# Sums of squares in a delta-rule encoder: two one-pass products of rounded parts in place of one full-precision product

## The chip, the cores and the metric

The kernel is one program on one core of a Trainium2 chip. The metric is the device time of one execution in microseconds (us). The engines are named as the profile names them: PE is TensorE (PEld its weight loads), DVE is VectorE, ACT is ScalarE, POOL is GpSimd, SP is SyncE.

## The reference

A two-layer encoder trunk over 512 positions of width 1024. Layer 1 has a gated DeltaNet with 8 heads of width 128, beside a cross-attention into 256 memory rows; layer 2 has sliding-window attention and the same cross-attention; each layer ends with a SwiGLU. What matters here is one head of the DeltaNet:

```python
qkv = silu(causal_depthwise_conv(qkv, conv_w))
q = l2_norm(q.reshape(B, S, 8, 128)) * 128 ** -0.5       # x * rsqrt(sum(x * x) + EPS)
k = l2_norm(k.reshape(B, S, 8, 128))
o = gated_delta_rule(q, k, v, g, beta)                   # chunks of 64, WY form
o = rms_norm(o, out_norm) * silu(z)                      # x * rsqrt(mean(x * x) + EPS)
```

Each head thus needs three sums of squares over its 128 channels for each of the 512 positions: of its keys, of its queries, and of its output.

## The kernel before

Activations lie with channels on the partitions and positions along the free axis, so a sum over channels is a product with a matrix of ones: `sq(ONES)` (128 by 128 ones, f32) times the squares (128x512, f32) gives the sum on every partition. The weight tiles of all projections come as a stream of blocks through a ring of four. ACT rounds a block to its upper part (`upper`, type fp32r), POOL subtracts for the lower part (`lower`), and PE makes three one-pass products for each 128-wide slice (`product`, line 594: upper by upper, upper weight by lower activation, lower weight by upper activation). A product of two f32 operands appears in the trace as two records for each instruction.

Each engine has its own program, written out by hand, and semaphores order them. Heads follow one another; PE does the delta rule of head h (`delta`, from line 696 on) and puts slices of the projections of head h+1 between its dependent steps: `fill(a, b)` stands for slices a to b-1 of the 32 (8 for each of q, k, v and gate), three one-pass products each. Head 7 has no next head; its only filling is the first memory-query tile, so `fill` does nothing there beyond slice 7.

Around the boundary of two heads PE's order is: in the loop over the four tiles of 128 positions (t = 0 to 3) the products of state and values, with the key sums of head h+1 (line 694) in tile 3; then `fill(30, 32)`; the output sums of head h (line 820); then, in the next `delta`, the query sums (line 703), four transposes of v (line 606, called from `delta`), two products with 64 rows that spread decay and beta over the partitions (line 717, "picks"), `fill(0, 2)`, four transposes of the normed keys (606 again), the keys' Gram product (line 727), `fill(2, 9)`, and the first step of the triangular inverse (line 735).

What feeds them: ACT squares k into `PM` (`square_k`) and q into `E0` (`square_q`), squares the output out of PSUM bank `D[5]` into `E1`, and takes Ln and Exp of the sums (`rr_k`, and in `delta`). Its Silu needs another table than Ln and Exp, so there is a table load behind `silu_v` (line 1326). DVE evacuates the value tiles in the t loop (`v_done`), updates `state` (`s_done`), then works on the output (`o_t1`), on the normed keys (`normed_k`, `kn_done`), on `PM` = keys times beta (`kb_done`, from the second pick), on the decay matrix (`dm_pre`) and on the first triangular factors (`z_done`). A helper's line stands for many operations: 1139 is ACT's `a`, 1578, 1581, 1584 and 1587 are DVE's multiply, subtract, fused operation and copy.

Of the kernel before, what the change touches and what calls it, by code (L numbers as in the profile page):

```python
# [126 lines left out]
def yoco_kernel(nc, x, mem, w_stream, w_out, w_down, w_ba, cols_in, squares_in, dist_in, out):  # L127
    with ExitStack() as ctx:
# [3 lines left out]
        def sem(name):  # L132
            return ctx.enter_context(nc.semaphore(name))
# [18 lines left out]
        class S:  # L152
# [48 lines left out]
            cv_conv = sem("cv_conv")  # L201
            c_ready = sem("c_ready")
            sz_done = sem("sz_done")
            sq_done = sem("sq_done")
            ss_done = sem("ss_done")
            rr_ln = sem("rr_ln")
# [35 lines left out]
            s_done = sem("s_done")  # L242
            o_done = sem("o_done")
            osq = sem("osq")
            oss = sem("oss")
            o_ln = sem("o_ln")
            o_rstd = sem("o_rstd")
# [66 lines left out]
        def due(n):  # L314

            return not isinstance(n, int) or n > 0
# [16 lines left out]
        def w(i):  # L333
            return ws[:, i, :]
# [4 lines left out]
        def sq(i):  # L339
            return sq_c[:, i, :]  # L340
# [26 lines left out]
        def psum(b, n=512):  # L367
            return bank[:, b, 0:n]
# [71 lines left out]
        def tz_count(k, g, first_only=False):  # L440

            if k < LEVELS - 2:
                return 2 * (k - 1) + g + 1
            if k == LEVELS - 2:
                return 2 * (LEVELS - 3) + 3 * g + (1 if first_only else 3)
            return 2 * (LEVELS - 3) + 6 + g + 1

        def row_cols(half):

# [135 lines left out]
        def _(pe):  # L585
# [110 lines left out]
            def delta(h, fill):  # L696

                if h == 0:
                    key_sums_dn(0)
                pe.wait_ge(S.sq_done, 2 * h + 2)  # L700
                if due(h):
                    pe.wait_ge(S.at_done, h)
                nc.tensor.matmul(psum(D[0]), sq(ONES), w(E0), start=True, stop=True).then_inc(S.ss_done, 1)
# [4 lines left out]
                transposes4(D[4], CV).then_inc(S.vtr_done, 1)  # L708

                if h == 0:  # L710
                    pe.wait_ge(S.rw_done, 2)
                    pe.wait_ge(S.pick_done, 1)
                if due(h):
                    pe.wait_ge(S.o_ln, h)
                    pe.wait_ge(S.v_done, NT * h)
                for half in range(2):
                    nc.tensor.matmul(psum(D[2 + half]), pick(h, half), rows(half), start=True, stop=True
                                     ).then_inc(S.gb_done, 1)
                fill(0, 2)
                pe.wait_ge(S.kn_done, h + 1)  # L720
                if due(h):
                    pe.wait_ge(S.o_t1, h)
# [414 lines left out]
        def _(act):  # L1137
            def a(out_, in_, func, **kw):
                return nc.scalar.activation(out_, in_, func, **kw)  # L1139
# [125 lines left out]
            def silu_v(h):  # L1265
                act.wait_ge(S.acc_free, TILE0["dn"] + 4 * h + 3)
                a(w(CV), w(CV), ACT.Silu).then_inc(S.c_ready, 1)

            def square_k(h):
                act.wait_ge(S.c_ready, 2 * h + 1)  # L1270
                if due(h):
                    act.wait_ge(S.tz_mm, 12 * h)
                a(w(PM), w(CK), ACT.Square).then_inc(S.sq_done, 1)

            def square_q(h):

                if due(h):
                    act.wait_ge(S.o_done, h)
                a(w(E0), w(CQ), ACT.Square).then_inc(S.sq_done, 1)

            def rr_k(h):
                act.wait_ge(S.ss_done, 2 * h + 1)
# [10 lines left out]
            def delta(h, fill, following):  # L1293
                act.wait_ge(S.gb_done, 2 * h + 1)
                a(w(EG), psum(D[2]), ACT.Exp).then_inc(S.eg_done, 1)
                act.wait_ge(S.ss_done, 2 * h + 2)
                a(w(E0), psum(D[0]), ACT.Ln, bias=col("eps")).then_inc(S.rr_ln, 1)
                at_once(act)
                act.wait_ge(S.dm_pre, h + 1)
                for t in range(NT):  # L1300
                    nc.scalar.activation(tt(DD, t), tt(DD, t), ACT.Exp, bias=dn(TMP1)[:, h, t:t + 1]
                                         ).then_inc(S.dm_done, 1)
                act.wait_ge(S.rr_ln, 2 * h + 2)
                a(psum(D[0]), w(E0), ACT.Exp, scale=-0.5, bias=col("ln_q")).then_inc(S.rr_done, 1)
# [269 lines left out]
        def _(dve):  # L1574
# [14 lines left out]
            def hi(tile_):  # L1589
                return act_hi[:, tile_, :].bitcast(F32)  # L1590
# [104 lines left out]
            def normed_k(h):  # L1695
                dve.wait_ge(S.rr_done, 2 * h + 1)
                mul(w(KN), w(CK), psum(D[1])).then_inc(S.kn_done, 1)

            def o_finish(h):
                dve.wait_ge(S.o_rstd, h + 1)  # L1700
                dve.wait_ge(S.o_t1, h + 1)
                mul(w(SZ), w(SZ), w(E1)).then_inc(S.o_t2, 1)

            def delta(h, fill, following=True):
# [66 lines left out]
                for t in range(NT):  # L1771
                    dve.wait_ge(S.v_mm, NT * h + t + 1)
                    cp(tt(E0, t), bank[:, D[3], 0:P]).then_inc(S.v_done, 1)
                    if t == NT - 1:
                        break
                    fill(2, t + 1)
                    dve.wait_ge(S.s_mm, 3 * h + t + 1)
                    if t == 0:
                        cp(state[:], bank[:, D[4], 0:P]).then_inc(S.s_done, 1)
                    else:  # L1780
                        dve.wait_ge(S.s_done, 3 * h + t)
                        stt(state[:], state[:], dn(GL)[:, h, t:t + 1], bank[:, D[4], 0:P], ALU.mult, ALU.add
                            ).then_inc(S.s_done, 1)
                fill(3)
                dve.wait_ge(S.osq, h + 1)
# [287 lines left out]
```

## Time and profile before

| | us |
|---|---|
| median of 3 runs (lowest, highest) | 1559.68 (1555.99, 1560.15) |
| the profiled execution, its own time | 1560.31 |
| its span, first to last instruction | 1558.5 |
| PE busy in the span | 1514.9 (97%) |
| DVE, ACT, POOL busy | 568.3, 601.8, 559.7 |
| mean granted clock of TensorE | 0.990 |

The span is 1.8 us shorter than the profiled execution's own time; differences are made in the span and carried to the median. Matmuls are pipelined: the start of one to the start of the next is what one costs, its own duration is longer than that.

### The profile page before, as it was taken

The page shows a single profiled execution, that of the slowest core. Times are in us where ns is not written, and L with a number is a line of the kernel's source. Part 1 is how long each engine was busy: PE and PEld are TensorE (multiplying, and loading weights), DVE is VectorE, ACT ScalarE, POOL GpSimd, SP SyncE. Part 2 cuts the span into 40 slices and gives each one's busy share as a digit, 9 for nine tenths or more (in the row PEclk, how much of TensorE's full clock was granted, in tenths as well). Part 3 has the DMA queues.
Part 4 walks back from the last instruction along what each step waited for, and adds up shares of the span by engine and source line. Part 5 has one row for each costly group of instructions (what it writes and reads, how often), then busy time and mean ns, then how long its engine had stood idle before and what let it go on. Part 6 is the DMA issues. An engine that isn't in the chain of part 4 may idle for free.

```text
span 1558.5 us, 23359 instructions
## 1 busy us (share of the span) xinstructions
PE 1514.9 (97%) x8956; PEld 1217.7 (78%) x8956; DVE 568.3 (36%) x1037; ACT 601.8 (39%) x998; POOL 559.7 (36%) x270
## 2 busy tenths in 40 slices
PE   6889999999999999999999999999999999999998
PEld 6867777777777788888888887777788888888887
DVE  2345556555564322221122224665432222112210
ACT  5534444334443433222232334675533232223221
POOL 4532221332312344444443443122244444444442
PEclk9999999999999999999999999999999999999999
DMA  6322101111101133223322233111123322332232
GB/s 238 119 66 70 42 29 54 55 55 42 49 15 31 53 113 108 101 71 103 117 88 102 68 118 102 41 38 31 41 81 109 108 92 83 110 107 83 91 86 80
DMA packets 39227, 124.36 MB, mean 80 GB/s; under 512 B 4192, under 2 KB 5472, under 8 KB 39136
## 3 DMA queue, kind: packets, MB, share of 16 engines
q1 hardware_dynamic: 38976, 122.81, 24.3%
q8 instruction: 66, 1.08, 0.3%
q10 hardware_dynamic: 160, 0.26, 0.1%
q14 instruction: 25, 0.20, 0.0%
HBM read 120.70 MB, written 2.10 MB: 79 GB/s over the span
## 4 chain that ended last, share of the span: by engine, by line
PE 93%; DVE 3%; ACT 2%; issue 1%; DMA 0%; POOL 0%; SPq 0%; DVEq 0%; ACTq 0%
PE bank L594 74%; ACT ws L1139 2%; PE bank L757 2%; PE bank L775 1%; PE bank L1073 1%; PE bank L778 1%; DVE act_lo L1584 1%; PE bank L940 1%; PE bank L899 1%; DVE ws L1587 1%; PE bank L1097 1%; PE bank L1084 1%; PE bank L740 1%; PE bank L812 1%; PE bank L786 1%
## 5 line engine op out<-in xcount | busy, mean ns | idle before, releaser
L541 POOL TENSOR_TENSOR w_lo<-w_raw,w_hi 128x1024 fp32r<-128x1024 f32 (+1 forms) x250 | 539.5, 2174 | 822.1 <-ACT w_hi L1139 822.0
L594 PE MATMUL bank<-act_hi,w_hi 128*128 128x512 f32 (+1 forms) x1776 | 711.5, 401 | 6.7 <-DVE act_lo L1584 2.6
L594 PE MATMUL bank<-act_hi,w_lo 128*128 128x512 f32 (+1 forms) x1776 | 681.7, 384 | 0.0
L594 PE MATMUL bank<-act_lo,w_hi 128*128 128x512 f32 (+1 forms) x1776 | 680.7, 383 | 0.0
L594 PEld LDWEIGHTS bank<-act_hi,w_hi 128*128 128x128 f32 x1776 | 336.3, 189 | 79.9 <-issue 13.2
L594 PEld LDWEIGHTS bank<-act_hi,w_lo 128*128 128x128 f32 x1776 | 336.1, 189 | 66.2
L594 PEld LDWEIGHTS bank<-act_lo,w_hi 128*128 128x128 f32 x1776 | 336.7, 190 | 62.3 <-issue 5.8
L1139 ACT ACTIVATE w_hi<-w_raw 128x1024 fp32r<-128x1024 f32 (+1 forms) x250 | 230.5, 953 | 88.8 <-PE bank L594 86.6
L1578 DVE TENSOR_TENSOR ws<-bank,ws 128x512 f32<-128x512 f32 x110 | 75.9, 690 | 336.9 <-PE bank L594 326.9
L1139 ACT ACTIVATE ws<-ws 128x512 f32<-128x512 f32 (+2 forms) x135 | 87.1, 647 | 155.4 <-DVE ws L1578 108.3
L1864 DVE TENSOR_TENSOR xT<-xT,bank 128x512 f32<-128x512 f32 (+1 forms) x48 | 33.0, 688 | 256.9 <-PE bank L594 256.9
L1139 ACT ACTIVATE act_hi<-ws 128x512 fp32r<-128x512 f32 (+1 forms) x52 | 32.8, 630 | 238.5 <-DVE ws L1578 238.5
L1139 ACT ACTIVATE ws<-bank 128x512 f32<-128x512 f32 (+2 forms) x64 | 41.8, 653 | 118.6 <-PE bank L991 44.9
L1587 DVE COPY ws<-bank 128x128 f32<-128x128 f32 (+4 forms) x94 | 40.0, 440 | 100.6 <-PE bank L594 51.7
L1242 ACT ACTIVATE ws<-bank,cols 128x512 f32<-128x512 f32 x24 | 16.5, 686 | 136.4 <-PE bank L594 136.4
L1584 DVE SCALAR_TENSOR_TENSOR ws<-bank,cols,ws 128x510 f32<-128x510 f32 (+3 forms) x80 | 59.6, 745 | 12.5 <-ACT ws L1242 10.8
L555 POOL TENSOR_TENSOR act_lo<-ws,act_hi 128x512 f32 (+1 forms) x8 | 10.3, 1291 | 148.6 <-ACT act_hi L1139 148.6
L1581 DVE TENSOR_TENSOR ws<-ws,bank 128x256 f32<-128x256 f32 (+2 forms) x112 | 39.3, 363 | 46.5 <-PE bank L778 44.3
L1139 ACT ACTIVATE ws<-xT 128x512 f32<-128x512 f32 (+1 forms) x24 | 15.2, 632 | 105.4 <-DVE xT L1864 105.4
L1139 ACT ACTIVATE ws<-bank,cols 128x512 f32<-128x512 f32 (+1 forms) x52 | 33.9, 651 | 51.0 <-PE bank L624 14.7
L1581 DVE TENSOR_TENSOR act_lo<-ws,act_hi 128x512 fp32r<-128x512 f32 (+1 forms) x44 | 30.5, 693 | 34.5 <-ACT act_hi L1139 34.5
L775 PEld LDWEIGHTS bank<-ws 64*64 64x64 f32 x640 | 31.8, 134 | 13.3 <-issue 12.8
(158 smaller groups left out, 1183.2 us busy)
## 6 DMA issues: line engine op xcount, KB each, us to landing
w_raw<-w_stream SPq DMA_DIRECT2D x154, 512.0 KB, 3.2
w_raw<-w_out SPq DMA_DIRECT2D x32, 384.0 KB, 3.1
w_raw<-w_down SPq DMA_DIRECT2D x32, 384.0 KB, 3.1
w_raw<-w_down SPq DMA_DIRECT2D x32, 320.0 KB, 3.1
ws<-x_in SPq DMA_DIRECT2D x1, 2048.0 KB, 8.4
ws<-mem_in SPq DMA_DIRECT2D x2, 512.0 KB, 4.8
out<-ws SPq DMA_DIRECT2D x1, 1024.0 KB, 4.2
out<-ws SPq DMA_DIRECT2D x1, 768.0 KB, 3.7
```

The costliest lines, as they stand in the source:

```text
L541: nc.gpsimd.tensor_tensor(w_lo[:, s, 0:width * P], w_raw[:, s, 0:width * P], w_hi[:, s, 0:width * P].bitcast(F32), ALU.subtract).then_inc( ...
L594: mm = nc.tensor.matmul(acc, wt[:, c % RING, wsl], at[:, act0(k0 + k), off:off + n], start=(start and k == 0 and m == 0), stop=(stop and k ...
L740: mm = nc.tensor.matmul(bank[:, D[0], t * P:(t + 1) * P], tt(KN, t), tt(QN, t), start=True, stop=True)
L757: mm = nc.tensor.matmul(bank[half_rows(r), D[3 - g], HB * i:HB * (i + 1)], diag(MM, t, r, r), packed(TT, t, r), start=True, stop=True)
L775: nc.tensor.matmul(bank[half_rows(r), D[4 + g], HB * i:HB * (i + 1)], packed(TT, t, r, 1), packed(PM, t, r), start=True, stop=True)
L1139: return nc.scalar.activation(out_, in_, func, **kw)
L1242: nc.scalar.activation(w(CQ + j), psum(j % 2), ACT.Copy, scale=conv_w(h, j, 3)).then_inc(S.cv_tap, 1)
L1578: return V.tensor_tensor(out_, x_, y_, ALU.mult)
L1581: return V.tensor_tensor(out_, x_, y_, ALU.subtract)
L1584: return V.scalar_tensor_tensor(out=out_, in0=x_, scalar=scalar, in1=y_, op0=op0, op1=op1)
L1587: return V.tensor_copy(out_, x_)
L1864: V.tensor_tensor(xT[:, k, :], xT[:, k, :], psum(j), ALU.add).then_inc(S.acc_free, 1)
```

## The change

For heads 1 to 7's keys and queries and for heads 0 to 6's output, squares are no longer multiplied in f32. ACT writes the squares into a PSUM bank, ACT copies them with rounding into an fp32r tile (the upper part), DVE subtracts that from the squares into a second fp32r tile (the lower part), and PE adds two one-pass products with a rounded matrix of ones. The keys' and the queries' parts share one pair of tiles. The query sums and the transposes of v move from the head's start to the end of the head before, ahead of the output sums; the picks move behind `fill(0, 2)`; `fill(2, 3)` moves between the key transposes and the Gram product. On ACT `square_q` moves ahead of `silu_v`. Head 0's sums and head 7's output sums are made as before.

```diff
+        SUM_T, OHI_T, OLO_T = KT + CAT - 1, 16, 17
+        ones_r = act_lo[:, 18, 0:P]
@@ tensor
+            def two_part_sums(acc, upper_, lower_):
+                nc.tensor.matmul(psum(acc), ones_r, upper_, start=True, stop=False)
+                return nc.tensor.matmul(psum(acc), ones_r, lower_, start=False, stop=True)
             def key_sums_dn(h):
                 pe.wait_ge(S.sq_done, 2 * h + 1)
-                nc.tensor.matmul(psum(D[1]), sq(ONES), w(PM), start=True, stop=True).then_inc(S.ss_done, 1)
...
+                two_part_sums(D[1], act_hi[:, SUM_T, :], act_lo[:, SUM_T, :]).then_inc(S.ss_done, 1)
+            def query_sums_dn(h):
                 pe.wait_ge(S.sq_done, 2 * h + 2)
...
+                two_part_sums(D[0], act_hi[:, SUM_T, :], act_lo[:, SUM_T, :]).then_inc(S.ss_done, 1)
+            def value_transposes(h):
                 pe.wait_ge(S.c_ready, 2 * h + 2)
                 if due(3 * h):
                     pe.wait_ge(S.s_done, 3 * h)
                 transposes4(D[4], CV).then_inc(S.vtr_done, 1)
+            def delta(h, fill):
+                if h == 0:
+                    key_sums_dn(0)
+                    query_sums_dn(0)
+                    value_transposes(0)
+                fill(0, 2)
                 if h == 0:
                     pe.wait_ge(S.rw_done, 2)
-                    pe.wait_ge(S.pick_done, 1)
+                    pe.wait_ge(S.pick_done, 2)
...
-                fill(0, 2)
                 pe.wait_ge(S.kn_done, h + 1)
...
                 transposes4(D[5], KN).then_inc(S.ktr_done, 1)
+                fill(2, 3)
...
-                fill(2, 9)
+                fill(3, 9)
...
                 fill(30, 32)
-                pe.wait_ge(S.osq, h + 1)
-                nc.tensor.matmul(psum(D[2]), sq(ONES), w(E1), start=True, stop=True).then_inc(S.oss, 1)
+                if h + 1 < DN_HEADS:
+                    query_sums_dn(h + 1)
+                    value_transposes(h + 1)
...
+                pe.wait_ge(S.osq_lo, h + 1)
+                two_part_sums(D[2], act_lo[:, OHI_T, :], act_lo[:, OLO_T, :]).then_inc(S.oss, 1)
@@ scalar
             def square_k(h):
...
+                act.wait_ge(S.tz_mm, 12 * h)
+                a(psum(D[1]), w(CK), ACT.Square).then_inc(S.sq_hi, 1)
+                act.wait_ge(S.sq_hi, 4 * h - 3)
+                act.wait_ge(S.ss_done, 2 * h)
+                a(act_hi[:, SUM_T, :], psum(D[1]), ACT.Copy).then_inc(S.sq_hi, 1)
             def square_q(h):
...
+                act.wait_ge(S.at_done, h)
+                a(psum(D[0]), w(CQ), ACT.Square).then_inc(S.sq_hi, 1)
+            def round_q(h):
+                act.wait_ge(S.sq_hi, 4 * h - 1)
+                act.wait_ge(S.ss_done, 2 * h + 1)
+                a(act_hi[:, SUM_T, :], psum(D[0]), ACT.Copy).then_inc(S.sq_hi, 1)
@@ scalar, delta
                 if following:
+                    square_q(h + 1)
                     silu_v(h + 1)
                 act.preload_act_table_set("natural_log_exp_and_others")
+                if following:
+                    round_q(h + 1)
                 act.wait_ge(S.o_done, h + 1)
-                a(w(E1), psum(D[5]), ACT.Square).then_inc(S.osq, 1)
                 if following:
-                    square_q(h + 1)
+                    a(psum(D[2]), psum(D[5]), ACT.Square).then_inc(S.osq, 1)
+                    act.wait_ge(S.osq, 2 * h + 1)
+                    a(act_lo[:, OHI_T, :], psum(D[2]), ACT.Copy).then_inc(S.osq, 1)
...
             conv_tile(0, 1)
+            a(ones_r, sq(ONES), ACT.Copy).then_inc(S.pick_done, 1)
@@ vector
+            def split_k(h):
+                dve.wait_ge(S.sq_hi, 4 * h - 2)
+                sub(act_lo[:, SUM_T, :], psum(D[1]), hi(SUM_T)).then_inc(S.sq_done, 1)
+            def split_q(h):
+                dve.wait_ge(S.sq_hi, 4 * h)
+                sub(act_lo[:, SUM_T, :], psum(D[0]), hi(SUM_T)).then_inc(S.sq_done, 1)
+            def split_o(h):
+                dve.wait_ge(S.osq, 2 * h + 2)
...
+                sub(act_lo[:, OLO_T, :], psum(D[2]), act_lo[:, OHI_T, :].bitcast(F32)).then_inc(S.osq_lo, 1)
@@ vector, delta, in and behind the loop over t
+                    if following and t == 1:
+                        split_k(h + 1)
+                if following:
+                    split_q(h + 1)
+                    split_o(h)
                 fill(3)
```

## Rows read from the trace of the kernel before

**Rows 1.** The page: the chain that ended last by engine, and two costly groups.
```profile
PE 93%; DVE 3%; ACT 2%; issue 1%; DMA 0%; POOL 0%; SPq 0%; DVEq 0%; ACTq 0%
...
L1139 ACT ACTIVATE act_hi<-ws 128x512 fp32r<-128x512 f32 (+1 forms) x52 | 32.8, 630 | 238.5 <-DVE ws L1578 238.5
...
L1581 DVE TENSOR_TENSOR act_lo<-ws,act_hi 128x512 fp32r<-128x512 f32 (+1 forms) x44 | 30.5, 693 | 34.5 <-ACT act_hi L1139 34.5
```

**Rows 2.** Busy time by stretch: PE, PEld, DVE, ACT, POOL, PE clock, DMA share, GB/s.
```profile
354.00:400.00 46.00, 45.94 (x444) 35.02 (x443) 26.24 (x61) 19.42 (x30) 11.93 (x6) 1.00 0.14 47
...
446.00:480.00 34.00, 30.76 (x367) 25.08 (x366) 20.38 (x52) 12.07 (x20) 2.49 (x2) 0.90 0.01 1
...
1080.00:1100.00 20.00, 18.48 (x92) 14.09 (x92) 6.81 (x11) 8.12 (x17) 4.90 (x2) 0.83 0.07 20
```

**Rows 3.** Timeline of PE across the boundary of heads 4 and 5: start, duration.
```profile
349.48 1.02 PE L694 MATMUL bank<-ws,sq_c 128*128 128x512 f32 x2
350.34 0.38 PE L802 MATMUL bank<-state,ws 128*128 128x128 f32 x2
...
351.49 0.39 PE L815 MATMUL bank<-ws 128*128 128x128 f32 x2
...
353.10 1.02 PE L820 MATMUL bank<-ws,sq_c 128*128 128x512 f32 x2
353.96 1.02 PE L703 MATMUL bank<-ws,sq_c 128*128 128x512 f32 x2
354.82 0.60 PE L606 MATMUL bank<-sq_c,ws 128*128 128x128 f32 x4
355.35 0.50 PE L717 MATMUL bank<-act_hi 64*128 64x512 f32 x2
355.78 0.50 PE L594 MATMUL bank<-act_hi,w_hi 128*128 128x512 f32 x1
356.12 0.39 PE L594 MATMUL bank<-act_lo,w_hi 128*128 128x512 f32 x1
...
357.27 0.60 PE L606 MATMUL bank<-sq_c,ws 128*128 128x128 f32 x4
357.71 1.06 PE L727 MATMUL bank<-ws 128*128 128x128 f32 x8
358.52 0.48 PE L594 MATMUL bank<-act_hi,w_hi 128*128 128x512 f32 x1
358.84 0.39 PE L594 MATMUL bank<-act_lo,w_hi 128*128 128x512 f32 x1
...
363.17 0.39 PE L594 MATMUL bank<-act_hi,w_lo 128*128 128x512 f32 x1
363.49 0.68 PE L735 MATMUL bank<-sq_c,ws 64*64 64x64 f32 x16
```

**Rows 4.** Timeline of ACT at the same boundary.
```profile
349.08 0.63 ACT L1139 ACTIVATE ws<-ws 128x512 f32<-128x512 f32 x1 [3.86 <-DVE ws L1584]
349.73 1.28 ACT L1326 ACT_TABLE_LOAD   x1
351.91 0.60 ACT L1139 ACTIVATE ws<-bank 128x512 f32<-128x512 f32 x1 [0.90 <-PE bank L815]
...
352.93 0.68 ACT L1139 ACTIVATE ws<-bank,cols 128x512 f32<-128x512 f32 x1
353.64 0.60 ACT L1139 ACTIVATE bank<-ws 128x512 f32<-128x512 f32 x1
```

**Rows 5.** Timeline of DVE at the same boundary.
```profile
346.84 0.35 DVE L1584 SCALAR_TENSOR_TENSOR state<-state,dn_s,bank 128x128 f32<-128x128 f32 x1 [0.29 <-PE bank L812]
348.09 0.29 DVE L1587 COPY ws<-bank 128x128 f32<-128x128 f32 x1 [0.91 <-PE bank L802]
...
356.00 0.69 DVE L1578 TENSOR_TENSOR ws<-ws,bank 128x512 f32<-128x512 f32 x1 [0.75 <-PE bank L717]
...
360.50 0.42 DVE L1581 TENSOR_TENSOR ws<-sq_c,bank 128x256 f32<-128x256 f32 x1
```

More of the change, by code:

```diff
@@ L203, in yoco_kernel @@
             sz_done = sem("sz_done")
+            sq_hi = sem("sq_hi")
             sq_done = sem("sq_done")
@@ L244, in yoco_kernel @@
             osq = sem("osq")
+            osq_lo = sem("osq_lo")
             oss = sem("oss")
@@ L689, in half_tiles @@
                 return range(NT // 2 * g, NT // 2 * (g + 1))
+            def two_part_sums(acc, upper_, lower_):
+                nc.tensor.matmul(psum(acc), ones_r, upper_, start=True, stop=False)
+                return nc.tensor.matmul(psum(acc), ones_r, lower_, start=False, stop=True)
             def key_sums_dn(h):
                 pe.wait_ge(S.sq_done, 2 * h + 1)
-                nc.tensor.matmul(psum(D[1]), sq(ONES), w(PM), start=True, stop=True).then_inc(S.ss_done, 1)
-            def delta(h, fill):
                 if h == 0:
-                    key_sums_dn(0)
+                    nc.tensor.matmul(psum(D[1]), sq(ONES), w(PM), start=True, stop=True).then_inc(S.ss_done, 1)
+                    return
+                two_part_sums(D[1], act_hi[:, SUM_T, :], act_lo[:, SUM_T, :]).then_inc(S.ss_done, 1)
+            def query_sums_dn(h):
                 pe.wait_ge(S.sq_done, 2 * h + 2)
-                if due(h):
-                    pe.wait_ge(S.at_done, h)
-                nc.tensor.matmul(psum(D[0]), sq(ONES), w(E0), start=True, stop=True).then_inc(S.ss_done, 1)
+                if h == 0:
+                    nc.tensor.matmul(psum(D[0]), sq(ONES), w(E0), start=True, stop=True).then_inc(S.ss_done, 1)
+                    return
+                two_part_sums(D[0], act_hi[:, SUM_T, :], act_lo[:, SUM_T, :]).then_inc(S.ss_done, 1)
+            def value_transposes(h):
                 pe.wait_ge(S.c_ready, 2 * h + 2)
@@ L708, in delta @@
                 transposes4(D[4], CV).then_inc(S.vtr_done, 1)
+            def delta(h, fill):
+                if h == 0:
+                    key_sums_dn(0)
+                    query_sums_dn(0)
+                    value_transposes(0)
+                fill(0, 2)
                 if h == 0:
                     pe.wait_ge(S.rw_done, 2)
-                    pe.wait_ge(S.pick_done, 1)
+                    pe.wait_ge(S.pick_done, 2)
                 if due(h):
@@ L817, in delta @@
                 fill(30, 32)
-                pe.wait_ge(S.osq, h + 1)
-                nc.tensor.matmul(psum(D[2]), sq(ONES), w(E1), start=True, stop=True).then_inc(S.oss, 1)
+                if h + 1 < DN_HEADS:
+                    query_sums_dn(h + 1)
+                    value_transposes(h + 1)
+                if h + 1 == DN_HEADS:
+                    pe.wait_ge(S.osq, 2 * h + 1)
+                    nc.tensor.matmul(psum(D[2]), sq(ONES), w(E1), start=True, stop=True).then_inc(S.oss, 1)
+                    return
+                pe.wait_ge(S.osq_lo, h + 1)
+                two_part_sums(D[2], act_lo[:, OHI_T, :], act_lo[:, OLO_T, :]).then_inc(S.oss, 1)
             proj_dn(0, 0)
@@ L1270, in square_k @@
                 act.wait_ge(S.c_ready, 2 * h + 1)
-                if due(h):
-                    act.wait_ge(S.tz_mm, 12 * h)
-                a(w(PM), w(CK), ACT.Square).then_inc(S.sq_done, 1)
-            def square_q(h):
-                if due(h):
-                    act.wait_ge(S.o_done, h)
-                a(w(E0), w(CQ), ACT.Square).then_inc(S.sq_done, 1)
+                if isinstance(h, int) and h == 0:
+                    a(w(PM), w(CK), ACT.Square).then_inc(S.sq_done, 1)
+                    return
+                act.wait_ge(S.tz_mm, 12 * h)
[3 more added lines that the diff above has]
+                a(act_hi[:, SUM_T, :], psum(D[1]), ACT.Copy).then_inc(S.sq_hi, 1)
+            def square_q(h):
+                if isinstance(h, int) and h == 0:
+                    a(w(E0), w(CQ), ACT.Square).then_inc(S.sq_done, 1)
+                    return
+                act.wait_ge(S.at_done, h)
[4 more added lines that the diff above has]
+                a(act_hi[:, SUM_T, :], psum(D[0]), ACT.Copy).then_inc(S.sq_hi, 1)
             def rr_k(h):
@@ L1324, in delta @@
                 if following:
+                    square_q(h + 1)
                     silu_v(h + 1)
                 act.preload_act_table_set("natural_log_exp_and_others")
+                if following:
+                    round_q(h + 1)
                 act.wait_ge(S.o_done, h + 1)
-                a(w(E1), psum(D[5]), ACT.Square).then_inc(S.osq, 1)
                 if following:
-                    square_q(h + 1)
+                    a(psum(D[2]), psum(D[5]), ACT.Square).then_inc(S.osq, 1)
+                    act.wait_ge(S.osq, 2 * h + 1)
+                    a(act_lo[:, OHI_T, :], psum(D[2]), ACT.Copy).then_inc(S.osq, 1)
+                else:
+                    a(w(E1), psum(D[5]), ACT.Square).then_inc(S.osq, 1)
+                if following:
                     rr_k(h + 1)
@@ L1697, in normed_k @@
                 mul(w(KN), w(CK), psum(D[1])).then_inc(S.kn_done, 1)
+            def split_k(h):
[6 more added lines that the diff above has]
+                dve.wait_ge(S.osq, 2 * h + 2)
+                if due(h):
+                    dve.wait_ge(S.oss, h)
+                sub(act_lo[:, OLO_T, :], psum(D[2]), act_lo[:, OHI_T, :].bitcast(F32)).then_inc(S.osq_lo, 1)
             def o_finish(h):
@@ L1783, in delta @@
                             ).then_inc(S.s_done, 1)
+                    if following and t == 1:
+                        split_k(h + 1)
+                if following:
+                    split_q(h + 1)
+                    split_o(h)
                 fill(3)
-                dve.wait_ge(S.osq, h + 1)
+                dve.wait_ge(S.osq, 2 * h + 1)
                 dve.wait_ge(S.sz_done, h + 1)
```

## The prediction

> **What bounds the kernel now.** I read the chain that ended last first: 93% of it lies on PE [rows 1]. Then busy time by stretch, to see whether that holds in the delta rule: in a stretch as long as one head PE is busy 45.94 of 46.00 us at a granted clock of 1.00, DVE 26.24 and ACT 19.42 [rows 2]. Then PE's timeline across the boundary of two heads, where the change sits; no row there shows idle time [rows 3]. So in heads 0 to 6 each 0.1 us taken off PE is gained, as long as nothing new arrives late. Head 7 is different: with little to fill in, PE is busy 30.76 of 34 us [rows 2]; its chain hangs on line 735, and PE is full up to there, so what is gained ahead of it counts.
>
> **PE, the three sums.** From the start of one f32 sum to the next instruction is 350.34 - 349.48, 353.96 - 353.10 and 354.82 - 353.96, each 0.86 us [rows 3]. A one-pass product of the same size: from 358.84 to 363.17 there are 19 steps, 4.33/19 = 0.228 us [rows 3]. Two are 0.455, so a sum gives back 0.405, three per boundary 1.215 us. There are seven boundaries.
>
> **PE, the changes of kind.** The first one-pass product after f32 work takes 358.84 - 358.52 = 0.32 us, 0.09 more than the others; after the picks with 64 rows it takes 356.12 - 355.78 = 0.34, 0.11 more; line 735, 64 rows, starts 0.32 after the last product, again 0.09; the v transposes ahead of the picks take 355.35 - 354.82 = 0.53, the same four of the keys ahead of f32 work 357.71 - 357.27 = 0.44, again 0.09. From one-pass work into f32 it costs nothing: 349.48 to 350.34 and 353.10 to 353.96 are equal, though only the second follows one-pass products [rows 3]. Counting the new order by these: new are the key sums between f32 products (0.09), the output sums after the v transposes (0.09), fill into picks (0.09), picks into key transposes (0.11, the nearest row is the one that leaves the picks), and key transposes into `fill(2, 3)` (0.09), together 0.47. Gone are transposes into picks (0.09) and picks into fill (0.11), 0.20. Net 0.27 lost per boundary, between 0.16 (leaving the picks into f32 free) and 0.38 (another 0.11 somewhere). A boundary gives 1.215 - 0.27 = 0.945, seven 6.6 us. Head 0 keeps its sums but has the new order: 0.09 + 0.09 + 0.11 + 0.09 - 0.20 = 0.18 lost. That leaves 6.4 us.
>
> **Queues and waits, on a clock of the row times.** Key sums: ACT sits idle for 3.86 us ahead of `silu_v` [rows 4], so the extra copy (0.63 by the fp32r group [rows 1]) costs nothing; the subtraction (0.69 by its group [rows 1]) comes behind the state update that ends at 347.19, ends at 347.9, and the next value copy was due at 348.09 [rows 5]. It fits by 0.2 us; if it did not, the key product with state behind it would be late by the same. PE wants it at 349.48. The key sums end 0.31 earlier than before (0.86 - 0.455 - 0.09), so everything behind them on PE stands 0.31 earlier: last output product 351.18, output sums' old place 352.79.
>
> Query sums: `square_q` is done long before. `round_q` can't start before the table load ends, 349.73 + 1.28 = 351.01 [rows 4]. Copy 0.60, subtraction 0.68 (the last value copy of DVE is done by then), hand-over 0.03 each (352.93 + 0.68 = 353.61, its dependent starts at 353.64 [rows 4]): ready at about 352.4. PE arrives at 352.79 and loads the weights of a product about one product ahead, 352.56. Covered by 0.2 us. Without that cover each 0.1 is lost seven times.
>
> Output sums: this is the tight one. The output was ready for ACT 351.91 - 351.49 = 0.42 after the start of line 815 [rows 3, 4], now 351.60. Square 0.60, copy 0.60, subtraction 0.69, three hand-overs of 0.03 to 0.05: 353.65 to 353.7. PE: 352.79 + 0.455 + 0.44 for the transposes = 353.68, the weight load a little earlier. I take 0.05 us of waiting per boundary, seven 0.35. Bounds: nothing (all covered), and 0.6 if each hand-over costs 0.16 (an estimate, five times the row), the two ACT operations cost the longest row, 0.68, and the weight load is exposed.
>
> Behind it: the sums land at 354.4, Ln takes 0.68, `o_ln` 355.15; PE reaches the picks at 355.7 and is not held. Key transposes at 356.2 need `kn_done`: `rr_k` slips behind the copy, 352.75 to 354.1, DVE does gate copy, `o_t1`, normed keys until 355.5. Free. The picks stand 0.37 later than before, so `kb_done` comes at 356.00 + 0.37 + 0.69 = 357.1 [rows 5]; the Gram product starts at 357.4, because `fill(2, 3)` stands ahead of it. The triangular start, before 360.50 + 0.42, slips to about 361.3; line 735, before 363.49, is reached at 362.45. So the cover of 2.6 us shrinks to 1.1 and holds, in head 7 too. The extra copy of ones sits on ACT at the start of the heads, off PE's path. No DMA moves; nothing is added on SP or POOL.
>
> **The sum.** 1560.31 - 6.4 + 0.35 = 1554.2 for the profiled execution's own time; the median of the runs is 0.63 below that execution, so 1553.6 us, 0.39% faster. What a measurement of this kernel can tell from no change is about 0.3%, 4.7 us.
>
> **A rule of the skill against the change.** The table load is a row of 1.28 us, and ACT is free when it ends: its next operation starts 0.90 us later, released by PE [rows 4]. The Trainium skill (ScalarE: Activation LUTs, "What ACT_TABLE_LOAD costs") gives about 1283 ns for the load and adds a drain of about 1380 ns to each switch of sets. If that drain came behind the load here, ACT would not be free before 352.39; the trace has it at work at 351.91, so the row speaks against it. By the rule both chains behind `round_q` would be late, see the third rival.
>
> **Rivals.**
> 1. The output chain is late by more than I say: 0.3 to 0.6 us of PE waiting at each boundary, 2.1 to 4.2 us in all. Then 1559.68 - 6.4 plus that, 1555.4 to 1557.5. For it: three dependent operations in place of one, with no slack. Against: the hand-overs in the rows are short. 18%.
> 2. The lower clock falls elsewhere. The stretch of head 7 has a mean clock of 0.90 over 34 us, the one from 1080 on 0.83 over 20 [rows 2]: each is 6.8 us at the 1.2 GHz level instead of 2.4, worth up to 3.4 us where PE is the bound. PE was busy 90% and 92% of these stretches, against all but 0.06 us in a head. Everything behind the heads moves by some 6 us, so one such place may vanish (1550.2, 7%) or one may be added (1557.0, 8%).
> 3. `round_q` waits for the end of ACT's change of tables longer than the row says. Place: the 0.90 us behind the load in each of seven boundaries. From 0.2 us on it is PE's wait for the query sums; at 1.4 us the query sums wait 1.2 and the output sums behind them 0.3 more, 10.5 us in all: 1563.8, slower by 0.26%. From about 0.9 us on the gain is gone. 2%.
> 4. The other side, by the clock: the new short waits of PE at the boundaries make the granted clock fall inside the heads, where it was 1.00 in the stretch shown and in the five like it [rows 2]. Price 3.4 us a time; with two the gain is gone, from four on (1567) it is slower by more than 0.3%. For it: head 7 shows that the clock does fall in this code once PE idles. Against: PE was busy 90% there, and the new waits are under 1% of a head. 5%.
> 5. The two products don't cost 0.455: an accumulating pair with weights of ones could take as long as f32 work. Then only the losses remain, about 1562. Line 594 is the same form of instruction and accumulates too, so 2%.
>
> **How the numbers follow.** My forecast, with its own range 1552.0 to 1555.5, 58%; rival 1 18%, rival 2 15%, rival 3 2%, rival 4 5%, rival 5 2%. Runs of one kernel spread over 4 us (1555.99 to 1560.15), which widens each. The range 1549.5 to 1558.8 takes in the forecast, rival 1 and most of rival 2, and leaves the slow cases and the far ends. Faster by over 0.3% (below 1555.0): most of the forecast, the better half of rival 2, a little of rival 1, 0.64. Within 0.3%: the rest of these and some of 3 to 5, 0.29. Slower 0.07.
>
> **What would show it.** Right: the sums as two records of 0.228 us from start to start; a head's period 0.9 to 1.0 us shorter; no waiting ahead of the query sums, up to 0.1 ahead of the output sums, with the lower part's subtraction named as releaser; line 735 not waiting. Wrong: a row of idle time on PE at the output sums of 0.3 or more, at the picks for the output's Ln, or at the Gram product for the keys times beta; a value copy of DVE in tile 2 that starts late behind the keys' subtraction; or a clock under 1.00 between 124 and 446 us.

## The result, and the profile after

The changed kernel takes 1549.83 us (median of 7 runs, 1542.53 to 1551.69), the kernel before 1559.57 in its 7 runs; the ratio is 0.993, with a 95% interval from 0.9918 to 0.9943. I forecast 1553.6, 6.1 us less; it is 9.7 less. By the ratio the time is 1548.8, a little under the low end of the range (1549.5). The profiled execution took 1550.04 us, span 1548.2. One run of a later version, `pair_twice` below, took 2148.07 us at a mean granted clock of 0.656 and is left out of its ratio.

In the timeline of PE of the changed kernel, line 756 is the old line 735, and lines 698 and 699 are the two products of a sum. These rows are the boundary of heads 4 and 5, and the line 756 of the head before:

```profile
312.80 0.68 PE L756 MATMUL bank<-sq_c,ws 64*64 64x64 f32 x16
...
344.03 0.38 PE L833 MATMUL bank<-ws 128*128 128x128 f32 x2
344.25 0.39 PE L836 MATMUL bank<-ws 128*128 128x128 f32 x2
344.47 0.39 PE L815 MATMUL bank<-ws 128*128 128x128 f32 x2
344.62 0.47 PE L698 MATMUL bank<-act_hi,act_lo 128*128 128x512 f32 x1
344.93 0.39 PE L699 MATMUL bank<-act_lo 128*128 128x512 f32 x1
345.16 0.38 PE L823 MATMUL bank<-state,ws 128*128 128x128 f32 x2
...
347.91 0.39 PE L698 MATMUL bank<-act_hi,act_lo 128*128 128x512 f32 x1
348.14 0.39 PE L699 MATMUL bank<-act_lo 128*128 128x512 f32 x1
348.38 0.60 PE L611 MATMUL bank<-sq_c,ws 128*128 128x128 f32 x4
348.74 0.50 PE L698 MATMUL bank<-act_lo 128*128 128x512 f32 x1
349.07 0.39 PE L699 MATMUL bank<-act_lo 128*128 128x512 f32 x1
349.31 0.39 PE L599 MATMUL bank<-act_hi,w_hi 128*128 128x512 f32 x1
...
350.46 0.39 PE L599 MATMUL bank<-act_hi,w_lo 128*128 128x512 f32 x1
350.78 0.50 PE L738 MATMUL bank<-act_hi 64*128 64x512 f32 x2
351.21 0.66 PE L611 MATMUL bank<-sq_c,ws 128*128 128x128 f32 x4
351.62 0.48 PE L599 MATMUL bank<-act_hi,w_hi 128*128 128x512 f32 x1
351.94 0.39 PE L599 MATMUL bank<-act_lo,w_hi 128*128 128x512 f32 x1
...
357.51 0.68 PE L756 MATMUL bank<-sq_c,ws 64*64 64x64 f32 x16
```

The head is 357.51 - 312.80 = 44.71 us long. Before, one head further on, it was 409.41 - 363.49 = 45.92, from the last row of [rows 3] to this one:

```profile
409.41 0.68 PE L735 MATMUL bank<-sq_c,ws 64*64 64x64 f32 x16
```

So a boundary gives back 1.21 us, not 0.9. No row of PE at the boundary has idle time. On ACT and DVE the new chain takes 2.00 us from the start of the output's square (346.74) to the start of the product on PE (348.74). The forecast's terms for it (0.60, 0.60, 0.69 and three hand-overs of 0.03 to 0.05) add up to 1.98 to 2.04.

```profile
344.30 0.63 ACT L1167 ACTIVATE ws<-ws 128x512 f32<-128x512 f32 x1 [2.77 <-DVE ws L1632]
344.95 1.28 ACT L1367 ACT_TABLE_LOAD   x1
346.24 0.60 ACT L1167 ACTIVATE act_hi<-bank 128x512 fp32r<-128x512 f32 x1
346.74 0.59 ACT L1167 ACTIVATE bank<-bank 128x512 f32<-128x512 f32 x1
347.36 0.60 ACT L1167 ACTIVATE act_lo<-bank 128x512 fp32r<-128x512 f32 x1
```

```profile
346.87 0.69 DVE L1629 TENSOR_TENSOR act_lo<-bank,act_hi 128x512 fp32r<-128x512 f32 x1 [1.00 <-ACT act_hi L1167]
347.99 0.69 DVE L1629 TENSOR_TENSOR act_lo<-bank,act_lo 128x512 fp32r<-128x512 f32 x1 [0.42 <-ACT act_lo L1167]
```

The output's lower part is ready at 347.99 + 0.69 = 348.68, and the first product of the output sums starts at 348.74. The table load starts 0.02 us behind the Silu ahead of it, and the copy that follows starts 0.01 us behind the load; the drain of some 1380 ns that the Trainium skill adds (ScalarE: Activation LUTs, "What ACT_TABLE_LOAD costs") does not show in this trace.

The difference of the two spans by stage, each from the same instruction in both timelines (the last start of a stage is the first of the next):

| stage | before | after | difference |
|---|---|---|---|
| start to the first sum of head 0 | 123.38 | 123.51 | +0.13 |
| from there to line 735 / 756 of head 0 | 10.51 | 10.45 | -0.06 |
| from there to the same line of head 7 | 320.78 | 312.32 | -8.46 |
| from there to the first memory scores | 32.45 | 30.62 | -1.83 |
| from there to the end | 1071.35 | 1071.34 | -0.01 |

The first line can't be put down to the change: the stage holds no edited product of PE, and its length lies between 120.6 and 124.5 us in the fourteen profiles of this document. The second is, since head 0 has the new order with its old sums:

```profile
123.38 1.12 PE L694 MATMUL bank<-ws,sq_c 128*128 128x512 f32 x2 [0.81 <-ACT ws L1139]
```

```profile
123.51 1.12 PE L705 MATMUL bank<-ws,sq_c 128*128 128x512 f32 x2 [0.81 <-ACT ws L1167]
...
133.96 0.68 PE L756 MATMUL bank<-sq_c,ws 64*64 64x64 f32 x16
```

The fourth line was not in the forecast's sum. PE's work there is the same; the clock is not. One row by stretch for the changed kernel, against the row of the same stretch in [rows 2] with its clock of 0.90:

```profile
446.00:480.00 34.00, 30.28 (x365) 23.65 (x364) 18.19 (x46) 10.96 (x16) 8.39 (x5) 1.00 0.04 11
```

### The profile page after: what moved, and what is told of

The parts are those of the page before. It is cut to its first block, busy times and chain, and to the rows that moved or that the text cites. A ratio compares the mean times of both kernels' runs of the same rounds, so it can differ in the third digit from the quotient of the medians.

```text
span 1548.2 us, 23430 instructions
## 1 busy us (share of the span) xinstructions
PE 1503.3 (97%) x8956; PEld 1212.6 (78%) x8956; DVE 581.3 (38%) x1058; ACT 613.2 (40%) x1020; POOL 559.7 (36%) x270
## 4 chain that ended last, share of the span: by engine, by line
PE 93%; DVE 3%; ACT 2%; issue 1%; DMA 0%; POOL 0%; SPq 0%; DVEq 0%; ACTq 0%
PE bank L599 74%; PE bank L778 2%; ACT ws L1167 2%; PE bank L796 2%; PE bank L1101 1%; PE bank L799 1%; DVE act_lo L1632 1%; PE bank L968 1%; PE bank L927 1%; DVE ws L1635 1%; PE bank L1125 1%; PE bank L761 1%; PE bank L611 1%; PE bank L919 1%; PE bank L957 1%
## 5 line engine op out<-in xcount | busy, mean ns | idle before, releaser
L1167 ACT ACTIVATE ws<-ws 128x512 f32<-128x512 f32 (+2 forms) x121 | 78.4, 650 | 147.8 <-DVE ws L1626 108.7
L1167 ACT ACTIVATE ws<-bank 128x512 f32<-128x512 f32 (+2 forms) x57 | 37.5, 659 | 107.9 <-PE bank L1019 44.9
```

## The experiments

Two questions: why a boundary gives 1.21 us, and whether head 7's clock belongs to the change. "Period" is the distance of line 735 or its counterpart from one head to the next. Where times are compared, note what the stages show below: kernels differ by several us in the time behind the heads, where nothing was edited. So the periods decide, not the ratios. A table behind the shifted versions has every version's distance from line 735 or its counterpart in head 0 to that in head 7, which is seven boundaries.

**The order alone** (`order_f32`). The sums are single f32 products again, the order is the new one. Query squares go to `E1`, output squares to `E0`, and DVE has no parts to make.

```diff
-                nc.tensor.matmul(psum(acc), ones_r, upper_, start=True, stop=False)
-                return nc.tensor.matmul(psum(acc), ones_r, lower_, start=False, stop=True)
+                return nc.tensor.matmul(psum(acc), sq(ONES), upper_, start=True, stop=True)
...
-                    a(psum(D[2]), psum(D[5]), ACT.Square).then_inc(S.osq, 1)
-                    act.wait_ge(S.osq, 2 * h + 1)
-                    a(act_lo[:, OHI_T, :], psum(D[2]), ACT.Copy).then_inc(S.osq, 1)
+                    a(w(E0), psum(D[5]), ACT.Square).then_inc(S.osq, 2)
```

> The new order of the boundary with all sums still single f32 products: query sums and v transposes ahead of the output sums, picks behind fill(0, 2), fill(2, 3) ahead of the Gram product, no parts. Theory A (a change from f32 to one-pass work costs 0.09 us, as the prediction counted): a boundary loses 0.09 (fill into picks) + 0.11 (picks into transposes) + 0.09 (key transposes into fill) - 0.20 = 0.09 or more, so 0.6 to 1.5 us slower in the heads, period 46.0 to 46.1 against 45.92. Theory B (the 0.09 of the first one-pass product is given back by the last f32 product before it, which gets shorter by as much): period within 0.03 of 45.92. Clock: if the dip in head 7 went away through the new order, head 7 shows a clock of 1.00 here too; if through the shorter heads or by chance, that is open.

Measured: ratio 0.9967 (0.9952 to 0.9983), period 45.85 to 45.90; over seven boundaries 320.46 us against 320.78, so 0.05 less for each than before, where theory A has 0.09 or more added. PE's timeline of this kernel; line 755 is the old 735:

```profile
317.65 0.68 PE L755 MATMUL bank<-sq_c,ws 64*64 64x64 f32 x16
...
354.46 1.02 PE L698 MATMUL bank<-ws,sq_c 128*128 128x512 f32 x2
354.92 0.80 PE L599 MATMUL bank<-act_hi,w_hi 128*128 128x512 f32 x1
355.56 0.40 PE L599 MATMUL bank<-act_lo,w_hi 128*128 128x512 f32 x1
...
363.50 0.68 PE L755 MATMUL bank<-sq_c,ws 64*64 64x64 f32 x16
```

Here an f32 sum is followed by one-pass work, and its rows say how such a place is to be read: 0.46 us to the next start, then 0.64 for the first one-pass product, together 1.10. An f32 sum ahead of f32 work takes 0.86 [rows 3] and a one-pass product 0.228, together 1.09. What the first one-pass product seems to take longer, the f32 instruction before it takes less. Theory A is excluded. Theory B gives its mechanism, but it expected the period within 0.03 of 45.92, and it is 0.02 to 0.07 below: the new order is a small gain of its own, taken apart further below.

**More changes of kind** (`kinds`).

```diff
                     mm = nc.tensor.matmul(bank[:, D[0], t * P:(t + 1) * P], tt(KN, t), tt(QN, t), start=True, stop=True)
+                    if t < NT - 1:
+                        fill(9 + t, 10 + t)
                 mm.then_inc(S.gg_done, 1)
-                fill(9, 12)
```

> The changed kernel with one edit: the four f32 products of keys with queries are no longer in a row with fill(9, 12) behind them, but each of the first three is followed by one slice of the fill. Same work, three more changes of kind to one-pass and three back, in each of heads 0 to 6. Theory A: each costs 0.09, a head 0.27, seven heads 1.9 us; period 44.99 against 44.72. Theory B: nothing, period within 0.05 of 44.72.

Measured: ratio 0.9937 (0.9922 to 0.9953), period 44.70 to 44.73, that of the changed kernel. PE's timeline, line 761 being the f32 products and 599 the slices between them:

```profile
315.26 0.39 PE L761 MATMUL bank<-ws 128*128 128x128 f32 x2
315.40 0.47 PE L599 MATMUL bank<-act_hi,w_hi 128*128 128x512 f32 x1
315.71 0.40 PE L599 MATMUL bank<-act_lo,w_hi 128*128 128x512 f32 x1
315.94 0.40 PE L599 MATMUL bank<-act_hi,w_lo 128*128 128x512 f32 x1
316.18 0.38 PE L761 MATMUL bank<-ws 128*128 128x128 f32 x2
```

The f32 product takes 0.14 and the first slice product 0.31; together 0.45, as 0.22 and 0.23 do apart. The expectation miscounts: without the edit the four products have `fill(9, 12)` behind them, which is one change to one-pass and one back, so the edit makes three of one, two more of each kind and not three. Theory A then has 0.18 for a head and a period of 44.90, which is still far from the 44.73 measured at most. Two more changes of this form cost nothing.

**Every pair twice** (`pair_twice`).

```diff
                 nc.tensor.matmul(psum(acc), ones_r, upper_, start=True, stop=False)
+                nc.tensor.matmul(psum(acc), ones_r, lower_, start=False, stop=True)
+                nc.tensor.matmul(psum(acc), ones_r, upper_, start=True, stop=False)
                 return nc.tensor.matmul(psum(acc), ones_r, lower_, start=False, stop=True)
```

> The changed kernel with each pair of one-pass products made twice (the first result is overwritten by the second). If a pair costs 0.455 us, a boundary gets 3 x 0.455 = 1.37 us longer, period 46.08, and the time 9.6 us longer than the changed kernel, about that of the kernel before. If an accumulating pair cost more (rival 5), more. If PE waited for the output parts and not for its own work, less than 0.455 would show at the output sums.

Measured: period 46.05 to 46.09, and 321.84 us over seven boundaries against 312.32, so 1.36 more for each than the changed kernel, or 0.45 for a pair. That is the forecast's price, and the accumulating pair is no dearer. The ratio is 0.9975 (0.9965 to 0.9985): by its heads this kernel is 1 us slower than before, yet it was timed faster, and only 6.1 us slower than the changed kernel (1555.57 against 1549.46), not 9.6. Its profiled execution had a mean granted clock of 0.997, that of the kernel before 0.990; that is the warning given above.

**The keys alone** (`keys_only`), on the kernel before.

```diff
+                pe.wait_ge(S.sq_k, h)
+                nc.tensor.matmul(psum(D[1]), ones_r, act_hi[:, SUM_T, :], start=True, stop=False)
+                nc.tensor.matmul(psum(D[1]), ones_r, act_lo[:, SUM_T, :], start=False, stop=True).then_inc(S.ss_done, 1)
```

> The kernel before with the key sums of heads 1 to 7 alone as two one-pass products of parts; order, query sums and output sums as before. As the products measured (0.86 against 0.455, changes of kind free): 0.40 per boundary, period 45.52, 2.8 us in all. By the prediction's count of kinds 0.31 per boundary, period 45.61.

Measured: period 45.51 to 45.54, and 318.00 us over seven boundaries against 320.78, so 0.40 for one sum per head; by the count of kinds it would have been 0.31. The ratio is 0.9947 (0.9929 to 0.9965), more than these 2.8 us; in the profile the rest lies behind the heads.

**The output's lower part later** (`late_output`).

```diff
+                    a(act_lo[:, OHI_T, :], psum(D[2]), ACT.Copy).then_inc(S.pick_done, 1)
+                    act.wait_ge(S.pick_done, h + 3)
                     a(act_lo[:, OHI_T, :], psum(D[2]), ACT.Copy).then_inc(S.osq, 1)
```

> The changed kernel with a second rounding copy of the output's squares in front of the first, so the lower part comes about 0.60 us later. My forecast gave this chain no cover (0.05 us of waiting), so PE should wait 0.55 to 0.65 ahead of the output sums: period 45.3 against 44.72, about 4 us. If a cover of x was there, the wait is 0.60 - x. If the chain is not on PE's path at all, no difference.

Measured: ratio 0.9952 (0.9936 to 0.9967), period 45.33 to 45.37, over seven boundaries 4.44 us more than the changed kernel, 0.63 for each. The copy and its hand-over are 0.63 to 0.64. PE's timeline of this kernel:

```profile
350.49 0.60 PE L611 MATMUL bank<-sq_c,ws 128*128 128x128 f32 x4
351.48 0.50 PE L698 MATMUL bank<-act_lo 128*128 128x512 f32 x1 [0.39 <-DVE act_lo L1631]
```

DVE's subtraction is named as releaser, and the whole delay comes through. The idle figure of 0.39 is smaller than the loss, since it counts from the modelled end of the transposes; from start to start it is 0.99 here and 0.36 in the changed kernel. So the output chain of the changed kernel had no cover at all. The delay alone doesn't show that it had no waiting; the rows of the changed kernel do, to 0.02 us. In head 0 the same transposes stand ahead of `fill(0, 2)`, which waits for no such chain, and the distance to the second one-pass product is 0.67, against 0.69 at the boundary (349.07 - 348.38):

```profile
125.33 0.60 PE L611 MATMUL bank<-sq_c,ws 128*128 128x128 f32 x4
125.68 0.48 PE L599 MATMUL bank<-act_hi,w_hi 128*128 128x512 f32 x1
126.00 0.40 PE L599 MATMUL bank<-act_lo,w_hi 128*128 128x512 f32 x1
```

**Both kernels again** (`after_again`, `before_again`), unedited.

> The changed kernel unchanged, for the clock of head 7 and the size of the gain. If the gain is the heads' alone, 8.4 us (0.54%); in the first profile the dip of the clock in head 7 had gone as well, 1.8 us more. If that is by chance, this profile may show the dip again (span 1550), if it belongs to the change, it is gone here too.

> The kernel before, unchanged, for the clock of head 7. If the dip of the clock there belongs to the kernel before, it shows again, with 1.8 us between line 735 of head 7 and the first memory scores (32.4 against 30.6). If it comes by chance, it may be gone, 30.6.

Measured: the changed kernel 1549.46 us, ratio 0.9932 (0.9919 to 0.9946), period 44.71, stage behind line 756 of head 7 30.62, clock there 1.00. The kernel before 1561.14 us in one run, period 45.92, that stage 32.20 (455.80 to 488.00), clock 0.90:

```profile
446.00:480.00 34.00, 31.60 (x370) 25.37 (x368) 21.05 (x52) 12.56 (x20) 2.49 (x2) 0.90 0.01 1
```

Up to here it looked like a property of the change. But `order_f32` (32.21), `keys_only` (32.49) and `late_output` (32.23) had the dip, `kinds` (30.62) and `pair_twice` (30.59) had none, and PE's work in head 7 is the same in all. `late_output` is the changed kernel but for one copy: with all its one-pass sums in place the dip is there.

**The same heads, a little later** (`before_shift1`, `before_shift2`, `after_shift1`, `after_shift2`). Products of the identity with itself, once, in head 0: 5 in the first of each pair, 10 in the second.

```diff
+                if h == 0:
+                    pe.wait_ge(S.mv_done, 2 * MEM_HEADS)
+                    for _ in range(5):
+                        nc.tensor.matmul(bank[:, D[5], 0:P], sq(IDENT), sq(IDENT), start=True, stop=True)
```

> The kernel before with 5 more f32 products of the identity with itself (about 1.1 us of PE) once, in head 0 ahead of the key transposes; heads 1 to 7 unchanged, only later. If the dip of the clock in head 7 belongs to the work of the heads before it, it stays (32.2 to 32.5 us from line 735 of head 7 to the first memory scores). If it hangs on when head 7 falls, it may vanish (30.6).

> The same with 10 products (about 2.2 us), heads 1 to 7 unchanged. Vanishing of the dip in one of the two shifts would show that timing decides and not the change's one-pass sums; the dip in both leaves the question open.

> The changed kernel with 5 such products in head 0. If the change's own work keeps the clock up in head 7, it stays up here. If timing decides, the dip may come back, with 1.6 to 1.9 us.

> The changed kernel with 10 such products in head 0 (about 2.2 us of PE). If the change's own work keeps the clock up in head 7, it stays up here too. If timing decides, the dip may come back, with 1.6 to 1.9 us.

Measured: 1559.42 and 1556.81 us for the two on the kernel before, 1543.84 and 1548.02 for the two on the changed one, a run each. The stage behind line 735 / 756 of head 7 takes 30.62, 30.63, 30.62 and 30.62: the dip is gone in the kernel before, with heads 1 to 7 as they were (period 45.92 and 45.93). The row of `before_shift2`:

```profile
446.00:480.00 34.00, 30.26 (x372) 23.53 (x371) 21.79 (x53) 13.17 (x22) 2.50 (x2) 1.00 0.01 1
```

So the one-pass sums are not needed to lose the dip: the same heads come with it and without. One difference is left in this comparison: `before_again` was profiled on another chip than the shifted versions, and no profile of the unedited kernel before is known to be from theirs. But `order_f32` ran on that chip too and has the dip, so the chip alone doesn't decide. Nor does the place in the span decide alone: line 735 of head 0 starts at 134.98 in `before_shift1`, without the dip, and at 135.04 in `before_again`, with it. The dip did not come back in the changed kernel. The tail moves as well: from the first memory scores of layer 1's stage to those of layer 2's `after_shift1` takes 598.9 us, the changed kernel 603.4. A stretch of this tail in the changed kernel, and then in `after_shift1`:

```profile
1060.00:1080.00 20.00, 16.73 (x108) 12.78 (x107) 7.64 (x14) 9.85 (x26) 2.69 (x2) 0.83 0.15 41
```

```profile
1060.00:1080.00 20.00, 16.73 (x98) 12.87 (x97) 8.53 (x14) 10.46 (x26) 2.58 (x1) 1.00 0.08 20
```

All profiles by stage, in us. "Head 0 to 7" runs from line 735 or its counterpart in head 0 to that of head 7, "head 7" from there to layer 1's first memory scores, "tail" from these to layer 2's. Behind each of the last two stands how much of it had a granted clock of 1.2 GHz:

| version | head 0 to 7 | head 7 | at 1.2 GHz | tail | at 1.2 GHz |
|---|---|---|---|---|---|
| before | 320.78 | 32.45 | 6.8 | 603.4 | 13.7 |
| `before_again` | 320.76 | 32.20 | 6.8 | 603.4 | 10.2 |
| `before_shift1` | 320.77 | 30.62 | 0 | 603.2 | 10.2 |
| `before_shift2` | 320.85 | 30.63 | 0 | 600.6 | 6.8 |
| `order_f32` | 320.46 | 32.21 | 6.8 | 600.5 | 6.8 |
| `keys_only` | 318.00 | 32.49 | 6.8 | 600.7 | 6.8 |
| `late_output` | 316.76 | 32.23 | 6.8 | 603.3 | 10.2 |
| `pair_twice` | 321.84 | 30.59 | 0 | 598.9 | 3.4 |
| `kinds` | 312.36 | 30.62 | 0 | 603.2 | 10.2 |
| `head7_filled` | 312.26 | 30.33 | 0 | 603.4 | 10.2 |
| changed | 312.32 | 30.62 | 0 | 603.4 | 10.2 |
| `after_again` | 312.25 | 30.62 | 0 | 603.1 | 10.2 |
| `after_shift1` | 312.27 | 30.62 | 0 | 598.9 | 3.4 |
| `after_shift2` | 312.33 | 30.62 | 0 | 599.0 | 3.4 |

The tail's length goes with its time at the lower clock: 598.9 or 599.0 us with 3.4 us of it, 600.5 to 600.7 with 6.8, 603.1 to 603.4 with more. The several us by which whole runs of these kernels differ beyond their heads are of this size, and no edit stands there.

**Head 7 filled** (`head7_filled`). The second memory-query tile's slices go into head 7's last steps.

```diff
-                mem_project(layer, 1, range(KT // 2 if layer else 0, KT))
+                if layer:
+                    mem_project(layer, 1, range(KT // 2, KT))
...
-            delta(DN_HEADS - 1, lambda first, end: mem_project(0, 0, range(first, min(end, KT))) if first < KT else None)
+            def beside_last_head(first, end):
+                if first < KT:
+                    mem_project(0, 0, range(first, min(end, KT)))
+                elif 22 <= first < 30:
+                    mem_project(0, 1, range(first - 22, first - 21))
+            delta(DN_HEADS - 1, beside_last_head)
```

> The changed kernel with the second memory-query tile's 8 slices (24 products, 5.5 us) moved from behind head 7 into its last steps (one slice at each fill place from 22 on), where PE waits for DVE. Those steps get longer by what the idle time doesn't hold: in the other heads a step of two slices takes 2.5 us, without them 2.0 to 2.1, so about 2 us for eight; behind it 5.5 are gone, but the chain from output sums over Ln, Exp and the normed query stands bare, 2 to 3 us. I expect 0.5 to 2 us less than the changed kernel from line 756 of head 7 to the first memory scores (30.6), and the clock at 1.00 through head 7. If the clock's dip came from too little work of PE, it can't come here.

Measured: 1549.72 us, ratio 0.9933 (0.992 to 0.9947), no better than the changed kernel. To the first scores it takes 30.33 us, 0.3 less, where 0.5 to 2 was expected. PE now waits for the normed query, and the clock falls behind that wait:

```profile
477.21 3.68 PE L927 MATMUL bank<-kmem,ws 128*128 128x256 f32 x8 [2.70 <-DVE ws L1638]
```

```profile
471.00:476.00 5.00, 2.82 (x9) 1.24 (x7) 1.48 (x3) 2.84 (x5) 0.00 (x0) 1.00 0.01 3
476.00:481.00 5.00, 3.79 (x9) 2.97 (x10) 1.43 (x3) 1.52 (x3) 3.97 (x3) 0.66 0.00 0
```

The scores take 3.5 us from start to start, where the kernel before has 1.72 (487.12 to 488.84). The idle time was moved, not removed. Of the versions tried none is faster than the changed kernel by its heads.

## Why the prediction was off

**Right.** PE as the bound of heads 0 to 6, and the three sums as the gain: 0.86 against 0.455 us was measured as 0.45 for a pair (`pair_twice`) and 0.40 for one sum exchanged (`keys_only`). The key sums' and the query sums' parts were in time. Rivals 3, 4 and 5 did not come: the copy starts 0.01 us behind the table load, the clock stays at 1.00 in the heads, the pair is not dearer. The output chain was just in time: `late_output` gives its cover as nothing, and the rows leave at most 0.02 of waiting where I took 0.05, so rival 1 was one short delay away. The forecast's time for it, 353.65 to 353.7, is an error of addition: 351.60 + 0.60 + 0.60 + 0.69 and three hand-overs of 0.03 to 0.05 make 353.58 to 353.64, just ahead of PE's 353.68, as measured. Line 735 does not wait.

**The failed step: "PE, the changes of kind".** I read 0.09 us off each first one-pass product behind f32 work, and counted net 0.27 per boundary and 0.18 in head 0, 2.1 us in all. Measured, the whole loss against 1.215 is about 0.01 per boundary (1.215 - 1.21), and in head 0 there is none: from its first sum to line 735 / 756 it takes 10.45 us, 0.06 less than before. The new order alone takes 0.05 off a boundary (`order_f32`), and the exchange of the sums then gives 320.46 - 312.32 = 8.14 us over seven boundaries, 0.39 for a sum where 0.405 was expected.

The rows were right and their reading wrong: where the first one-pass product takes longer, the f32 instruction before it takes less, and I counted the first and not the second. Taken over both instructions where an f32 one stands ahead, the five new changes cost this, against the 0.47 that I counted:

| new change | distances | cost | forecast |
|---|---|---|---|
| key sums between f32 products | 0.15 + 0.31 + 0.23, against 0.22 + 0.455 | 0.01 | 0.09 |
| output sums behind the v transposes | 0.36 + 0.33, against 0.44 + 0.23 | 0.03 | 0.09 |
| fill into picks | 0.32, against 0.23 | 0.09 | 0.09 |
| picks into key transposes | 0.43, against 0.43 | 0.00 | 0.11 |
| key transposes into `fill(2, 3)` | 0.41 + 0.32, against 0.44 + 0.23 | 0.06 | 0.09 |

Together that is 0.19, about the 0.20 that is gone. So not every change is free: that from one-pass products into the picks with 64 rows has its full 0.09, and the two behind transposes keep a part. The pair was to be seen ahead of the prediction. In [rows 3] the four f32 products of the Gram line take 358.52 - 357.71 = 0.81 ahead of one-pass work, where four at 0.22 make 0.88, and the kernel before has an f32 sum ahead of one-pass work behind head 7, with 0.46 and then 0.64:

```profile
488.84 1.02 PE L891 MATMUL bank<-ws,sq_c 128*128 128x512 f32 x2
489.30 0.80 PE L594 MATMUL bank<-act_hi,w_hi 128*128 128x512 f32 x1
489.94 0.40 PE L594 MATMUL bank<-act_lo,w_hi 128*128 128x512 f32 x1
```

I never added up an f32 instruction and its successor.

**The missing term: head 7's clock.** The forecast's sum took head 7 as it was. Its dip went away, 1.83 us. That is rival 2, one place vanishing, which I had at 7% and at 3.4 us; the price was too high, by my reading because PE is not the bound in all of that stage, which no run tests. In the tail, 6.8 us more at the lower clock go with 4.5 us more in all (the changed kernel against `after_shift1`), so half the stretch is not an upper bound everywhere. That the dip is not tied to the kind of the sums is shown from both sides: the shifted versions of the kernel before have f32 sums and no dip, `late_output` has one-pass sums and the dip. What decides it stays open, and so does whether the changed kernel avoids it by more than chance: in the six profiles with a period of 44.7 (the first one, `after_again`, `kinds`, `head7_filled` and the two shifts) the clock holds through head 7's state products, in two unedited profiles of the kernel before it falls, and two shifts of each kernel are too few to say more. That it hangs on where head 7 stands against the earlier stretches at the lower clock is a guess, which was not tested.

**The size.** 8.46 us in the heads and 1.83 behind them, less 0.07 ahead of them, are the 10.2 between the two profiled spans (1558.47 and 1548.24). In the runs it is 9.7 beside the first seven and 10.8 beside the second set; that difference is of the size of the tail's. `order_f32` and `keys_only` were timed 3 to 5 us better than their heads are, and `pair_twice` nearly 6 us better (4.7 faster than the kernel before by the medians, 1.06 slower by its heads), which is more than the 4.7 us (0.3%) that I took for what a measurement of this kernel can tell.

## What to carry to other kernels

Where PE is the bound and an f32 product has a constant operand that rounds exactly, two one-pass products of upper and lower parts give back nearly half, if the extra copy and subtraction find room on the other engines: here each of three chains fitted, one with no cover at all. Price a change of order by the distance from one fixed instruction to another over the whole group, never by the one row that looks longer. And when stretches at a lower clock lie elsewhere in the kernel, compare by stage, since the total moved by several us here without any edit there.

## What was not expected of the hardware

- In the records of PE, at a change from f32 to one-pass work, the last f32 instruction appears short (0.14 for 0.22, 0.46 for 0.86) and the next one long (0.31 for 0.23, 0.64 for 0.23); the sum is that of the two apart. Behind transposes it is 0.03 to 0.06 more.
- Four f32 transposes of one form read 0.36, 0.41, 0.44 or 0.53 us from their start to the next, by what stands behind them.
- A dip of the clock from 2.4 to 1.2 GHz in head 7 cost 1.6 to 1.9 us (32.2 to 32.5 against 30.6), and came and went with PE's work in heads 1 to 7 unchanged. In the tail, 6.8 us more at 1.2 GHz went with 4.5 us (603.4 against 598.9).
